# Three raw slots in the out-projection stage, and one adaLN load moved into the main ring

## Time and profile before

| | us |
|---|---|
| median of three runs | 1197.24 (1196.52 to 1200.06) |
| the profiled execution | 1197.26 |
| its span | 1195.4 |
| TensorE busy | 1114.2 (93%) |
| VectorE busy | 536.1 (45%) |
| ScalarE busy | 366.3 (31%) |
| median time from issue to landing, expert loads of the ring | 20.3 to 20.9 |
| the same, out-projection loads of ScalarE's queue | 8.9 |

### The profile page before, as it was taken

The page is one execution under the profiler, slowest core; times in us unless marked ns, Lnnn a source line. Parts: engine busy times, 40 slices in busy tenths (PEclk is TensorE's granted clock), DMA queues, the critical chain, the costliest instruction groups (busy, mean ns, idle before and its releaser), DMA issues.

```text
span 1195.4 us, 14481 instructions
## 1 busy us (share of the span) xinstructions
PE 1114.2 (93%) x5577; PEld 682.1 (57%) x5577; DVE 536.1 (45%) x781; ACT 366.3 (31%) x526; POOL 54.7 (5%) x100
## 2 busy tenths in 40 slices
PE   4899999999999999999999999999899888988795
PEld 1666766777777677667788874434344234423231
DVE  0464575555455444454466755241415041504056
ACT  3342342544433333333445533320112001201023
POOL 0210100110000220000010100000000000000000
PEclk9999999999999999999999999999999999999998
DMA  9999978887777898988898799999999999999994
GB/s 356 385 385 380 362 286 320 313 300 283 286 288 284 306 350 323 327 298 315 330 363 260 221 389 421 374 422 422 424 424 423 424 422 422 424 423 422 424 406 173
DMA packets 114965, 423.22 MB, mean 354 GB/s; under 512 B 9089, under 2 KB 9265, under 8 KB 82641
## 3 DMA queue, kind: packets, MB, share of 16 engines
q1 hardware_dynamic: 101968, 389.57, 83.2%
q0 software_dynamic: 5424, 15.35, 4.9%
q10 hardware_dynamic: 7504, 17.37, 4.0%
HBM read 418.27 MB, written 3.98 MB: 353 GB/s over the span
## 4 chain that ended last, share of the span: by engine, by line
PE 70%; DMA 26%; DVE 1%; SPq 1%; issue 1%; ACT 1%; DVEq 0%
PE bank L825 14%; PE bank L826 13%; PE bank L827 13%; PE bank L1194 12%; DMA mraw<-in_w_exp_up 10%; PE bank L806 5%; DMA raw<-in_w_in 4%; DMA mraw<-in_w_exp_gate 4%; DMA mraw<-in_w_exp_down 3%; PE bank L1233 3%; PE bank L1133 2%; DMA raw<-in_w_ada 2%; DMA mraw_y<-in_w_exp_gate 2%; DMA araw<-in_w_ada 2%; PE bank L1275 1%; PE bank L790 1%
## 5 line engine op out<-in xcount | busy, mean ns | idle before, releaser
L1719 DVE TENSOR_TENSOR w_lo<-raw,w_hi 128x1024 fp32r<-128x1024 f32 x192 | 232.0, 1223 | 246.6 <-ACT w_hi L1368 245.7
L1368 ACT ACTIVATE w_hi<-raw 128x1024 fp32r<-128x1024 f32 x192 | 200.4, 1057 | 313.9 <-DMA raw<-in_w_in 160.8
L825 PE MATMUL bank<-w_hi,h_hi 128*128 128x512 f32 x512 | 206.2, 403 | 5.2 <-DVE w_lo L1719 4.4
L826 PE MATMUL bank<-w_lo,h_hi 128*128 128x512 f32 x512 | 200.0, 391 | 0.0
L827 PE MATMUL bank<-w_hi,h_lo 128*128 128x512 f32 x512 | 199.8, 390 | 0.0
L1194 PE MATMUL bank<-mraw,xg 128*64 128x512 f32 x720 | 184.9, 597 | 13.3 <-DMA mraw<-in_w_exp_gate 6.2
L825 PEld LDWEIGHTS bank<-w_hi,h_hi 128*128 128x128 f32 x512 | 96.2, 188 | 45.7 <-issue 24.8
L1194 PEld LDWEIGHTS bank<-mraw,xg 128*64 128x64 f32 x720 | 57.6, 136 | 109.2 <-issue 104.7
L827 PEld LDWEIGHTS bank<-w_hi,h_lo 128*128 128x128 f32 x512 | 96.1, 188 | 21.0
L826 PEld LDWEIGHTS bank<-w_lo,h_hi 128*128 128x128 f32 x512 | 96.3, 188 | 18.1
L2185 DVE SCALAR_TENSOR_TENSOR d_lo<-bank,slot_w,d_hi 128x512 fp32r<-128x512 f32 x32 | 23.9, 747 | 160.2 <-ACT d_hi L1667 159.5
(11 more groups left out here) (293 smaller groups left out, 1323.6 us busy)
## 6 DMA issues: line engine op xcount, KB each, us to landing
raw<-in_w_in SPq DMA_DIRECT2D x64, 1024.0 KB, 8.4
raw<-in_w_ada SPq DMA_DIRECT2D x60, 1024.0 KB, 8.5
mraw<-in_w_exp_gate SPq DMA_DIRECT2D x46, 1024.0 KB, 20.9
mraw<-in_w_exp_up SPq DMA_DIRECT2D x44, 1024.0 KB, 20.9
mraw<-in_w_exp_down SPq DMA_DIRECT2D x42, 1024.0 KB, 20.3
araw<-in_w_ada SPq DMA_DIRECT2D x64, 512.0 KB, 10.8
raw<-in_w_out ACTq DMA_DIRECT2D x12, 1024.0 KB, 8.9
raw<-in_w_na_o SPq DMA_DIRECT2D x8, 1024.0 KB, 7.1
```

The source lines that it names most:

```text
L825: nc.tensor.matmul(o, hi[:, k, s], wh, start=k == first, stop=False)
L826: nc.tensor.matmul(o, hi[:, k, s], wl, start=False, stop=False)
L1368: nc.scalar.activation(w_hi[:, u % AHEAD], r, ACT.Copy).then_inc(hi_ready, 1)
L1719: v.tensor_tensor(w_lo[:, u % AHEAD], r, w_hi[:, u % AHEAD].bitcast(F32), ALU.subtract).then_inc(raw_done[n % RAW], 4)
```

## The change

LATE_ADA becomes 3, so adaLN load 92 enters the ring at l = 78, and its product is run on TensorE in the middle of l = 78 (alone). From ring position `RING_CUT` (that of d80) on, the loads go round slots 0 to 2 alone. Slot 3's last user is adaLN load 92; after its product SyncE issues expert load 7 into it, right behind expert load 12 and ahead of load 8. The three late adaLN loads 93, 94 and 95 use slots 2, 0 and 1, and expert loads 4, 5 and 6 follow them. Every `n % RAW` and `n // RAW` becomes `ring_slot(n)` and `ring_turn(n)`. ScalarE's issue stays at iteration l for d(l + 4).

```diff
@@ -345,7 +345,7 @@
-        LATE_ADA = 4
+        LATE_ADA = 3
@@ -357,9 +357,24 @@
+        RING_CUT = DENSE_AT[L_OUT]
+        ring_slots = [n % RAW if n < RING_CUT else (n - RING_CUT + RING_CUT % RAW) % (RAW - 1) for n in range(RING_LOADS)]
+
+        def ring_slot(n):
+
+            return ring_slots[n]
+
+        def ring_turn(n):
+
+            return ring_slots[:n].count(ring_slots[n])
+
+        def slot_end(slot):
+
+            return 8 * ring_slots.count(slot)
+
         def landed_count(n):
 
-            return 16 * (n // RAW) + 16
+            return 16 * ring_turn(n) + 16
@@ -472,16 +487,16 @@
         def slot_released(queue, n):
 
-            if n >= RAW:
-                queue.wait_ge(raw_done[n % RAW], 8 * (n // RAW))
+            if ring_turn(n):
+                queue.wait_ge(raw_done[ring_slot(n)], 8 * ring_turn(n))
...
@@ -496,8 +511,8 @@
-            queue.dma_start(raw[:, n % RAW], view[:, LOAD_K * quad:LOAD_K * quad + LOAD_K, col:col + COL]
-                            ).then_inc(raw_landed[n % RAW], 16)
+            queue.dma_start(raw[:, ring_slot(n)], view[:, LOAD_K * quad:LOAD_K * quad + LOAD_K, col:col + COL]
+                            ).then_inc(raw_landed[ring_slot(n)], 16)
@@ -580,6 +595,8 @@
                 first_gate_up_load(14)
                 sp.wait_ge(chunk_read, reads(21))
                 first_gate_up_load(12)
+                sp.wait_ge(raw_done[RAW - 1], slot_end(RAW - 1))
+                first_gate_up_load(2 * RAW - 1)
                 sp.wait_ge(unit_used, 2 * L_ALL - 4)
                 first_gate_up_load(8)
@@ -589,8 +606,8 @@
-                for n in range(RAW):
-                    sp.wait_ge(raw_done[n], 8 * (RING_LOADS // RAW))
+                for n in range(RAW - 1):
+                    sp.wait_ge(raw_done[n], slot_end(n))
                     first_gate_up_load(RAW + n)
@@ -1099,8 +1116,7 @@
-            for a in (92, 93):
-                ada_super(a)
+            ada_super(93)
             pe.wait_ge(chosen_ready, 1)
...
```

More of the change, by code:

```diff
@@ L482, in ada_super_load @@
             slot_released(queue, n)
-            queue.dma_start(raw[:, n % RAW].rearrange("p (a k) n -> p a (k n)", a=1),
-                            ada_v[:, k:k + 1, super_chunk * D:(super_chunk + 1) * D]).then_inc(raw_landed[n % RAW], 16)
+            queue.dma_start(raw[:, ring_slot(n)].rearrange("p (a k) n -> p a (k n)", a=1),
+                            ada_v[:, k:k + 1, super_chunk * D:(super_chunk + 1) * D]).then_inc(raw_landed[ring_slot(n)], 16)
         def dense_load(queue, l):
@@ L803, in ada_super @@
                         pe.wait_ge(ada_evac, super_chunk - GATE1)
-                pe.wait_ge(raw_landed[n % RAW], landed_count(n))
+                pe.wait_ge(raw_landed[ring_slot(n)], landed_count(n))
                 for g in range(4):
-                    last = nc.tensor.matmul(bank[7][32 * g:32 * g + 32], cpad[:, k], raw[:, n % RAW, g],
+                    last = nc.tensor.matmul(bank[7][32 * g:32 * g + 32], cpad[:, k], raw[:, ring_slot(n), g],
                                             start=k == 0, stop=k == KD - 1)
-                last.then_inc(raw_done[n % RAW], 8)
+                last.then_inc(raw_done[ring_slot(n)], 8)
             def unit(l, half):
@@ L817, in unit @@
                           (o_hi, o_lo) if (chunk - 8) % 4 == 2 else (f_hi, f_lo))
-                pe.wait_ge(raw_done[n % RAW], 8 * (n // RAW) + 4 * half + 4)
+                pe.wait_ge(raw_done[ring_slot(n)], 8 * ring_turn(n) + 4 * half + 4)
                 for t in range(UNIT_K):
@@ L833, in last_load @@
                 n = DENSE_AT[l]
-                pe.wait_ge(raw_done[n % RAW], 8 * (n // RAW) + 8)
+                pe.wait_ge(raw_done[ring_slot(n)], 8 * ring_turn(n) + 8)
                 for s in range(NS):
@@ L1363, in high @@
                 if u % 2 == 0:
-                    act.wait_ge(raw_landed[n % RAW], landed_count(n))
+                    act.wait_ge(raw_landed[ring_slot(n)], landed_count(n))
                 if u >= AHEAD:
                     act.wait_ge(unit_used, u - AHEAD + 1)
-                r = raw[:, n % RAW, (u % 2) * UNIT_K:(u % 2) * UNIT_K + UNIT_K]
+                r = raw[:, ring_slot(n), (u % 2) * UNIT_K:(u % 2) * UNIT_K + UNIT_K]
                 nc.scalar.activation(w_hi[:, u % AHEAD], r, ACT.Copy).then_inc(hi_ready, 1)
@@ L1444, in super_done @@
                 n = ADA_AT[A_SUPER + KD * (super_chunk - GATE1) + KD - 1]
-                act.wait_ge(raw_done[n % RAW], 8 * (n // RAW) + 8)
+                act.wait_ge(raw_done[ring_slot(n)], 8 * ring_turn(n) + 8)
             def evac_mod_rows(super_chunk, n):
@@ L1717, in low @@
                 dve.wait_ge(hi_ready, u + 1)
-                r = raw[:, n % RAW, (u % 2) * UNIT_K:(u % 2) * UNIT_K + UNIT_K]
+                r = raw[:, ring_slot(n), (u % 2) * UNIT_K:(u % 2) * UNIT_K + UNIT_K]
                 v.tensor_tensor(w_lo[:, u % AHEAD], r, w_hi[:, u % AHEAD].bitcast(F32), ALU.subtract
-                                ).then_inc(raw_done[n % RAW], 4)
+                                ).then_inc(raw_done[ring_slot(n)], 4)
             def chained(ins):
@@ L2113, in _ @@
             n = ADA_AT[95]
-            dve.wait_ge(raw_done[n % RAW], 8 * (n // RAW) + 8)
+            dve.wait_ge(raw_done[ring_slot(n)], 8 * ring_turn(n) + 8)
             dve.wait_ge(bias2_row_in, 64)
```

## The result

The changed kernel takes 1206.1 us (median of 4 runs, 1205.54 to 1207.67), the kernel before on the same chip 1197.36; the ratio is 1.0072, 95% interval 1.0055 to 1.0089. It is slower by 8.7 us; 7.3 were forecast. That is inside the stated range (1198.0 to 1207.5), and just above the forecast's own case (1203 to 1206). The profiled execution has a span of 1203.9 us against 1195.4.

A forecast was written before the change was run, and what follows sets the result against it. TensorE was taken to bound the kernel until about 829 us, then DMA. Terms 0 + 1.0 + 5.2 + 1.1 = +7.3 us gave 1204.6 us, with a range of 1198.0 to 1207.5.

The forecast's parts named there:

- the forecast's own case: Whole program: late d84 stalls TensorE, total +7.3 us to 1204.6; case range 1203 to 1206, chance 0.58.
- 2 MiB out of the full stretch: DMA ahead of the hole: two loads leave, worth 5.0 us of DMA time, but counted at 0 for the end.
- The hole: DMA gap at 748 to 752 us, ended by TensorE's read of place 8; to grow from about 3 to 8 us.
- Product 92: TensorE at l = 78: the moved adaLN product delays what follows by 1.0 us; leaving its old place returns nothing.
- SyncE's and ScalarE's waits: Both load queues: d83 waits until 607.6 us with four expert loads behind it; d84 is issued at 613.0.
- d84's landing: Out-projection stage: dense load 84 shares DMA with expert and x loads and lands at 636.4 us, 5.3 past 631.1.
- the stall: TensorE in the out-projection stage: reaches d84 at 633.5, can start only at 638.8 us, +5.2 us.
- three-way round: DMA during d84's transfer: three queues take turns packet by packet, 44.3 ns a round; 382 rounds take 16.9 us.
- The slack of 5.7 us: Out-projection stage: d84 may land 5.7 us late, by 631.1, before TensorE stands.
- x1 transposes: TensorE after d84's column: transposes wait for VectorE's column chunk until 645.3 instead of 644.2 us, +1.1 us.
- The hidden lateness: Rival, d84's transfer: landing by 631.1 means TensorE never stands, only product 92's 1.0 us left, 1198.3; chance 0.27.
- The faster case: Rival, loads after 750 us: if they could start earlier, -5.0 and +1.0 us give 1193.2; chance 0.05.

The follow-up runs named there:

- kernel 9: The kernel before with the first gate pair of experts 2 and 3 loading half its bytes, 1 MiB less ahead of the hole: 1197.53 us, ratio 1.0007.
- Kernel 2: The kernel before with LATE_ADA = 3 alone: four slots, no early expert load, product 92 at l = 78: 1200.35 us, ratio 1.0021.
- kernel 8: The changed kernel with expert loads 13, 14, 12 and 7 issued one at a time, plus four unread filler matmuls in the routing: 1197.61 us, ratio 1.0004.
- kernel 1: The changed kernel with expert load 7 issued at its old place behind loads 4 to 6, three slots kept: 1201.83 us, ratio 1.0036.
- kernel 3: The changed kernel with SyncE issuing expert loads 13, 14 and 12 ahead of dense loads d82 and d83: 1200.68 us, ratio 1.0023.
- kernel 5: The kernel before with product 92 moved alone (four slots), plus four unread filler matmuls ahead of product 93: 1197.93 us.
- kernel 7: The kernel before with four unread filler matmuls between products 92 and 93: 1197.56 us, against 1197.11 for the kernel before.
- kernel 4: The changed kernel with four extra matmuls, never read, behind product 93 in the routing: 1204.27 us.
- kernel 11: The changed kernel with expert loads 13, 14, 12 and 7 issued one at a time, without filler matmuls: 1199.71 us, ratio 1.0022.

## Why the prediction was right, point by point

- *2 MiB out of the full stretch, 0.* Right, and shown: the hole grew, kernel 9 gained nothing, and the table holds for all kernels. The hole itself grew less than forecast: the DMA time missing in it went from 3.0 us (748 to 753) to 6.6 (753 to 762), not to 8. Some of the rest lies ahead of it, at 712 to 716, with a share of 0.83 where the kernel before has 1.01.
- *Product 92, +1.0.* Measured 1.23 in the profile, at the upper bound. Kernel 2, whose TensorE never waits in the out-projection stage, differs from the kernel before by this and by the clock alone.
- *SyncE's and ScalarE's waits.* The low half that d83 waited for ended at 608.2 (forecast 607.6), and that for d84 at 613.62 (613.0). Both are late by the 0.40 us by which this profile ran late in general and the 0.23 by which the product was undersized. The expert loads follow from 608.78. Waits of three slots that are hidden: confirmed by kernel 8.
- *d84's landing, 636.4, and the stall, +5.2.* It landed at 635.4 and the stall was 3.8. The mechanism is shown by the queue rows and by kernels 1, 3 and 8. The size was off by 1.4 us: TensorE came there 0.6 us later than forecast, which costs nothing more, and d84 was ready 0.8 us earlier. The step that was mis-sized is the length of a three-way round once the row fetches follow the x loads: they were priced at 19 ns a packet, from a window of the kernel before in which they ran beside one queue. In the changed kernel the rounds of 628 to 630 us (packets, MB, share of the 2 us) have them at 0.237 x 2000 / 56 = 8.5 ns:

```profile
q1 hardware_dynamic: 58, 0.48, 58.1%
q0 software_dynamic: 56, 0.16, 23.7%
q10 hardware_dynamic: 58, 0.12, 16.4%
```

  A round there is 2000 / 58 = 34 ns, not 44. When the expert queue was empty, at about 631.0, 130 packets of d84 were left, as forecast, but the 382 rounds since 617.2 had taken 13.8 us, not 16.9. Against that, d84's first packets came 1.3 us later than forecast, and its landing followed some 1.3 us behind its last packets, not 0.4; so it landed 1.0 us before the forecast time. The slack of 5.7 us and the 2.4 us from high half to TensorE came out (635.42 to 637.95).
- *x1 transposes, +1.1.* In the changed kernel 0, hidden by the slow clock; in kernel 1, without it, 1.37.
- *What the sum lacked.* 1.74 us behind the stall, nearly all of it half clock, and 1.48 us in the routing. The total came near by two errors of opposite sign, 2.5 us too much for the stall and its wake and 3.2 us of clock not seen, and that nearness is luck. The forecast counted idle time as the whole price of idle time, and counted product 92's old place as worth nothing. In a run where the clock falls there, that place was worth something. Nor do time differences between runs come from waits and instructions alone: the clock was full in the profiled run of the kernel before, not in all its runs.
- *The rivals.* The hidden lateness would have given 1198.3; kernel 8, where it holds, has 1197.61. The Trainium skill's fit that the prediction quotes for this rival (DMA: Bandwidth & Descriptors, Anatomy of one DMA) is made on DMAs that GpSimd issues; d84 is one of ScalarE's, and with no expert load beside it, in kernel 8, it still took 8.2 us, not 4.4. The faster case needed a MiB ahead of the hole to count, and kernel 9 excludes it.

No version that moves all its bytes beats the kernel before. Kernels 5, 7 and 8 are not told apart from it.

## What to carry to other kernels

In this kernel a prefetch out of a saturated stretch was worth nothing, since a wait for a consumer stood between. So find the last hole in the DMA's share and ask what releases the load behind it; here 1 MiB less ahead of it gained nothing, and 1 MiB less behind it about its full DMA time. When a wait moves an in-order queue's loads, look at what they will meet: queues share by packets, so a transfer with small packets beside two with large ones can take more than twice its time (21.7 us here, against 8.2), though its own size and slot are untouched. And price a stall of TensorE with the half clock that may follow it, not with its idle time alone.

## What the runs showed of the hardware that was not expected

- Behind an idle time of 3.8 us the granted clock fell to 0.50, the 1.2 GHz level, just as TensorE began again, for some 3.3 us; its 512-column matmuls then came every 0.43 us, not 0.23. In kernel 4 (3.7 us idle) it fell 1.6 us before TensorE began again and stayed at half for 5.2 us behind that. In kernel 1 (1.1 and 1.4 us idle) it did not fall.
- In the routing the clock fell with TensorE busy in the windows before (router matmuls of 20 columns, transposes, adaLN products of 32 rows), in the profiled runs of the changed kernel and of kernels 2, 3, 7 and 11, not in the other profiled ones. In the changed kernel it cost 1.5 us. What decides it in a run stays open. But it goes with the spread of the kernel before (1195.4 to 1201.4 us, one execution of 3967.7 left out): its 15 runs with a mean clock of at most 0.991 have spans of 1197.0 to 1199.4 us, its 56 runs with 0.993 or more 1193.6 to 1196.0. The medians differ by 3.4 us. Where in the run the clock fell is known for the profiled ones alone.
- The same 1 MiB load d84 took 8.2, 11.8, 15.4, 17.7, 19.0 and 21.7 us to land in kernel 8, the kernel before, and kernels 2, 3, 1 and the changed one, by what else was queued with it.
